# Root at the outputs for two attention linears and the expert queries, and modulation sums moved between linears

## The reference

```python
def rms_norm(x, g):
    y = xf * lax.rsqrt(jnp.mean(xf * xf, axis=-1, keepdims=True) + EPS)
    return y * g
def modulate(h, shift, scale):
    return h * (1 + scale[:, None, :]) + shift[:, None, :]
...
mod = c_act @ ada_w[layer] + ada_b[layer]            # nine vectors: shift, scale, gate three times
h = modulate(rms_norm(x, norm_g[layer, 1]), sh2, sc2)
qkv = h @ w_qkv                                      # layer 0; layer 1 has h @ w_q alone
...
# expert layer, h = rms_norm_2(x, norm_peer_g)
q = jnp.einsum('bsd,dq->bsq', h, w_pq).reshape(b, s, PEER_HEADS, 2, PEER_HALF)
sub_scores = jnp.einsum('bshpc,pnc->bshpn', q, subkeys)
top_s, top_i = lax.top_k(sub_scores, 16)             # then the best 16 of the 16 x 16 pairs, and a softmax
act = jax.nn.gelu(jnp.einsum('chkd,cd->chk', u_sel, hc)) * gc
out = jnp.einsum('chk,chkd->cd', act, v_sel)
```

## Time and profile before

| | us |
|---|---|
| median of 3 runs | 2206.01 (2204.38 to 2207.89) |
| the profiled execution, its own time | 2206.66 |
| its span, first to last instruction | 2204.8 |
| PE busy | 1933.1 (88%) |
| DVE busy | 1680.7 (76%) |
| ACT busy | 878.7 (40%) |
| POOL busy | 531.1 (24%) |
| mean granted TensorE clock | 0.932 of full |

### The profile page before, as it was taken

The page is one execution under the profiler, slowest core; times in us unless marked ns, Lnnn a source line. Parts: engine busy times, 40 slices in busy tenths (PEclk is TensorE's granted clock), DMA queues, the critical chain, the costliest instruction groups (busy, mean ns, idle before and its releaser), DMA issues.

```text
span 2204.8 us, 33666 instructions
## 1 busy us (share of the span) xinstructions
PE 1933.1 (88%) x12770; PEld 1636.5 (74%) x12770; DVE 1680.7 (76%) x2959; ACT 878.7 (40%) x1415; POOL 531.1 (24%) x467
## 2 busy tenths in 40 slices
PE   6999997999999999899999999989876676766766
PEld 6999995999999999699999999979622222222222
DVE  6876877887778768774569998648887787887765
ACT  3444446544454444654545444655321211212111
POOL 0110001211102110111120001423565544445441
PEclk7999996999999999899999999999998888888888
DMA  7878770577848777245444454424999999999996
GB/s 315 309 281 333 298 268 20 192 306 278 288 159 308 282 259 296 81 173 191 154 169 172 174 190 173 172 96 155 390 422 422 422 422 423 422 422 423 422 423 268
DMA packets 88358, 604.80 MB, mean 274 GB/s; under 512 B 9715, under 2 KB 11011, under 8 KB 21036
## 3 DMA queue, kind: packets, MB, share of 16 engines
q1 hardware_dynamic: 37276, 243.46, 30.6%
q0 software_dynamic: 37040, 270.57, 29.5%
q10 hardware_dynamic: 13920, 89.15, 10.4%
HBM read 599.96 MB, written 3.18 MB: 274 GB/s over the span
## 4 chain that ended last, share of the span: by engine, by line
PE 29%; DMA 21%; DVE 7%; ACT 2%; issue 1%; DVEq 0%; ACTq 0%; POOLq 0%
DMA row_pair<-in_peer_uv,mod_ring 21%; PE ps L760 20%; PE ps L1172 3%; PE ps L791 3%; DVE row_pair L2362 2%; DVE w_lo L1708 1%; DVE work L1775 1%; ACT w_hi L1194 1%; PE ps L868 0%; PE ps L986 0%; ACT diag L1675 0%; DVE work L2139 0%; PE ps L823 0%; PE ps L973 0%; DVE work L1963 0%
## 5 line engine op out<-in xcount | busy, mean ns | idle before, releaser
L1708 DVE TENSOR_TENSOR w_lo<-raw,w_hi 128x2048 fp32r<-128x2048 f32 (+1 forms) x248 | 525.5, 2121 | 219.9 <-ACT w_hi L1194 219.3
L1172 PE MATMUL ps<-row_pair,diag 128*128 128x512 f32 x768 | 429.9, 720 | 192.5 <-ACT diag L1675 192.5
L760 PE MATMUL ps<-HH,w_hi 128*128 128x256 f32 x2032 | 575.7, 283 | 1.0 <-DVE w_lo L1708 1.0
L760 PE MATMUL ps<-HL,w_hi 128*128 128x256 f32 x2032 | 571.4, 281 | 0.0
L760 PE MATMUL ps<-HH,w_lo 128*128 128x256 f32 x2032 | 569.1, 280 | 0.0
L1194 ACT ACTIVATE w_hi<-raw 128x2048 fp32r<-128x2048 f32 (+1 forms) x248 | 439.9, 1776 | 264.7 <-PE ps L760 219.8
L1172 PEld LDWEIGHTS ps<-row_pair,diag 128*128 128x128 f32 x768 | 171.2, 230 | 450.5 <-ACT diag L1675 244.3
L2362 DVE SCALAR_TENSOR_TENSOR row_pair<-row_pair,HTOK 128x1024 f32<-128x1024 f32 x256 | 313.7, 1226 | 131.5 <-DMA row_pair<-in_peer_uv,mod_ring 129.3
L733 POOL DMA_INDIRECT row_pair<-in_peer_uv,mod_ring x256 | 318.4, 1244 | 326.1 <-PE ps L1172 261.1
L760 PEld LDWEIGHTS ps<-HH,w_lo 128*128 128x128 f32 x2032 | 383.3, 189 | 0.0
L760 PEld LDWEIGHTS ps<-HL,w_hi 128*128 128x128 f32 x2032 | 382.9, 188 | 0.0
(11 more groups left out here) (311 smaller groups left out, 2926.0 us busy)
## 6 DMA issues: line engine op xcount, KB each, us to landing
raw<-in_f_in SPq DMA_DIRECT2D x88, 1024.0 KB, 4.9
mod_ring<-in_ada ACTq DMA_DIRECT2D x74, 1024.0 KB, 6.6
raw<-in_f_out SPq DMA_DIRECT2D x64, 704.0 KB, 5.0
raw<-in_mix_a SPq DMA_DIRECT2D x16, 1024.0 KB, 4.8
raw<-in_mix_g SPq DMA_DIRECT2D x8, 1024.0 KB, 4.8
raw<-in_pq SPq DMA_DIRECT2D x8, 1024.0 KB, 4.8
first<-in_ada ACTq DMA_DIRECT2D x4, 1024.0 KB, 11.0
raw<-in_a_q SPq DMA_DIRECT2D x4, 1024.0 KB, 7.9
```

Of the source, the lines that this page charges most:

```text
L760: ins = mm(out_, ops[1] if left else ops[0], ops[0] if left else ops[1], start=(first and k == k0 and n == 0), stop=(last and k == k1 - 1 ...
L1172: last = mm(ps[:, 2 * t + c, :], diag[:, d, :], row_v(k)[:, c * 512:(c + 1) * 512], start=False, stop=False)
L1708: v.tensor_tensor(slot(w_lo, g), slot(raw, g), f32(slot(w_hi, g)), ALU.subtract).then_inc(low["v"], 1)
```

## The change

a_q and b_q become raw linears. Their raw tiles are made in `ffn` (with gain/8, which stands for the factor on the queries) and lie in the buffers HH and HL, which the normalised chunks then overwrite one by one, each after tile 1 has read it (`raw_read`). Their outputs are scaled by the new `raw_scale` on DVE, and ACT adds the shift (`raw_take`). The end of `ffn` has no norm sum of its own any more.

The modulation tiles move: 28 and 29 to a_q's tiles 2 and 3, 30 to 33 to a_k, 34 and 35 to a_v, 76 and 77 to b_q's tiles 2 and 3, 78 and 79 to b_o; the sums and takes follow. The loads of the subkeys and the memory on SP's queue move from ahead of f11_in's first tile to behind its third (they wait for the last modulation sum). In s_v, the last two outputs are taken ahead of the last chunk's high and low part. Attention B's small buffer `decay0` moves to the root's place.

In pq all eight tiles run on x times the weight. The sums of squares are made per token (`token_sums`), root and reciprocal are two columns `RT`, and the scores are scaled with them as ACT copies them (L1635). Only x is turned to token-major form; `HTOK` becomes x times `RT` times the weight row, which SP loads twice by broadcast once x_o is done, ahead of pq's tile 3. The cross-attention's output has its parts in EH and EL instead of HH and HL. All of pq is taken by ACT.

```diff
@@ -575,8 +584,16 @@
-            def ffn(w_in, w_out):
+            def memory():
+                sp.wait_ge(mods_ready, summed(ADA_TILES // 2 - 1))
+                sp.dma_start(subk[:, :, :], a["subkT"]).then_inc(sub_loaded, 16)
+                sp.dma_start(MEM, a["memT"]).then_inc(mem_loaded, 16)
+            def ffn(w_in, w_out, late=None):
                 tiles(w_in, 0, RING)
+                if late is not None:
+                    late()
...
@@ -591,12 +608,15 @@
             tiles("b_o")
-            sp.wait_ge(mods_ready, summed(ADA_TILES // 2 - 1))
-            sp.dma_start(subk[:, :, :], a["subkT"]).then_inc(sub_loaded, 16)
-            sp.dma_start(MEM, a["memT"]).then_inc(mem_loaded, 16)
...
+            ffn("f11_in", "f11_out", late=memory)
...
+            tiles("pq", 0, 3)
+            sp.wait_ge(units_done, LIN["x_o"].unit_end)
+            for t in range(TT):
+                sp.dma_start(HTOK[:, t, :], a["norm_peer_row"].partition_broadcast(P).rearrange("q a n -> q (a n)")
+                             ).then_inc(gpeer_loaded, 16)
+            tiles("pq", 3, 5)
...
@@ -713,11 +732,9 @@
                 if n == 1:
-                    pool.wait_ge(hl_ready, SET["n11"] + DC)
-                if n == 2:
+                    pool.wait_ge(el_ready, ESET["attX"] + DC)
+                if n == 3:
                     pool.wait_ge(tok_turned, 4)
-                if n == 3:
-                    pool.wait_ge(tok_turned, 8)
...
@@ -1028,12 +1042,14 @@
+            raw_tile("a_q", 0, 1, mid=lambda: norm_sum(1))
+            raw_tile("a_q", 1, 1, mid=lambda: mod_sum(13))
+            for t in range(2, 4):
+                feat_tile("a_q", t, new="n1", raw=True)
             for t in range(4):
-                feat_tile("a_q", t, new="n1", mid=(lambda: mod_sum(14)) if t == 2 else None)
+                feat_tile("a_k", t, mid=(lambda: mod_sum(14 + t // 2)) if t % 2 == 0 else None)
             for t in range(4):
-                feat_tile("a_k", t, mid=(lambda: mod_sum(15 + t // 2)) if t % 2 == 0 else None)
-            for t in range(4):
-                tok_tile("a_v", t, mid=(lambda: mod_sum(17)) if t == 0 else None)
+                tok_tile("a_v", t, mid=(lambda: mod_sum(16 + t // 2)) if t % 2 == 0 else None)
...
@@ -1068,14 +1084,17 @@
             ffn(2, "f10_in", "f10_out", "n4", 5, 56)
-            for t in range(4):
-                feat_tile("b_q", t, new="n5", mid=(lambda: mod_sum(38)) if t == 2 else None)
-            mod_sum(39)
+            raw_tile("b_q", 0, 5, mid=lambda: norm_sum(5))
+            raw_tile("b_q", 1, 5, mid=lambda: mod_sum(37))
+            for t in range(2, 4):
+                feat_tile("b_q", t, new="n5", raw=True)
             pe.wait_ge(freed["d"], LIN["b_q"].freed_d)
-            pe.wait_ge(mods_ready, summed(ADA_TILES // 2 - 1))
+            pe.wait_ge(mods_ready, summed(37))
             pe.wait_ge(attn_ready, STEP_END["B"])
+            mod_sum(38)
             residual("b_o", "attB", 6)
+            mod_sum(39)
...
-            raw_tile("pq", 0, N_PEER, mid=lambda: norm_sum(N_PEER))
-            raw_tile("pq", 1, N_PEER)
-            head_scores(0)
-            tok_turns(0)
-            for t in range(2, 8):
-                feat_tile("pq", t, new="n11", raw=True, mid=(lambda: head_scores(t - 1)) if t > 2 else None)
-                if t == 2:
-                    head_scores(1)
-                if t < 5:
+            def token_sums():
+                ks = [k for k in range(DC) if not 0 < k < PRE]
+                pe.wait_ge(presum_ready, PRESUM[N_PEER])
+                pe.wait_ge(squares_ready, 8 * RANK[N_PEER] + DC)
+                for t in range(TT):
+                    for k in ks:
+                        last = mm(ps_token[:, t:t + 1], SQ[:, k, t * P:(t + 1) * P], ones[:, 0:1],
+                                  start=(k == ks[0]), stop=(k == ks[-1]))
+                last.then_inc(sumsq_ready, 1)
+            raw_tile("pq", 0, N_PEER, mid=token_sums)
+            for t in range(1, 8):
+                feat_tile("pq", t, mid=lambda: head_scores(t - 1))
+                if t <= TT:
-            pe.wait_ge(tok_ready, 8)
+            pe.wait_ge(tok_ready, 4)
...
@@ -1250,10 +1284,15 @@
                     act.wait_ge(t_ready, 8 * n + k + 1)
+                    if n in EIGHTH and k < DC - 1:
+                        act.wait_ge(raw_read, (DC - 1) * EIGHTH.index(n) + k + 1)
+                    if n in EIGHTH and k == DC - 1:
+                        act.wait_ge(units_done, CHUNK_UNIT[LIN["a_q" if n == 1 else "b_q"].chunk0 + 3])
                         act.wait_ge(units_done, LIN["s_v"].unit_end)
+                        take("s_v", 6, VS[:, 0, 3 * 256:4 * 256])
...
@@ -1461,22 +1500,28 @@
+            split(LIN["a_q"].tile0 + 2)
             shift_high("n1", 1)
+            split(LIN["a_q"].tile0 + 3)
             for t in range(4):
-                split(LIN["a_q"].tile0 + t + 2)
-                if t:
-                    load_mod(28 + t + 1)
+                if t > 1:
+                    split(LIN["a_q"].tile0 + t + 2)
+                if t == 3:
+                    load_mod(30)
                     q = 2 * t + m
-                    take("a_q", q, QT[:, q, :], scale=HD ** -0.5)
+                    if t < RAW_TILES:
+                        raw_take(1, t, q, QT[:, q, :]).then_inc(freed["a"], 1)
+                    else:
+                        take("a_q", q, QT[:, q, :], scale=HD ** -0.5)
                 split(LIN["a_k"].tile0 + t + 2)
-                load_mod(32 + t + 1)
+                load_mod(31 + t)
                 split(LIN["a_v"].tile0 + t + 2)
-                if t == 0:
-                    load_mod(37)
+                if t < 3:
+                    load_mod(35 + t)
...
@@ -1624,37 +1677,31 @@
             split(LIN["pq"].tile0 + 2)
-            norm_root(N_PEER)
-            norm_high(N_PEER)
-            split(LIN["pq"].tile0 + 3)
+            act.wait_ge(sumsq_ready, RANK[N_PEER] + 1)
+            f(RT, ps_token, ACT.Sqrt, scale=1.0 / D, bias=eps[:, :]).then_inc(token_root, 1)
                     f(S[t][:, 2 * h:2 * h + 2, :].rearrange("p a n -> p (a n)"), ps[:, SUBKEY_BANK[t], 0:2 * NK],
-                      ACT.Copy).then_inc(s_ready, 1)
+                      ACT.Copy, scale=RT[:, t:t + 1]).then_inc(s_ready, 1)
-                dst, t = (HTOK, XTOK)[j // 2], j % 2
                     act.wait_ge(tok_turned, 2 * j + half + 1)
-                    f(dst[:, t, half * 512:(half + 1) * 512], ps[:, SUBKEY_BANK[half], :], ACT.Copy).then_inc(tok_ready, 1)
-            sub_copies(0)
-            split(LIN["pq"].tile0 + 4)
-            tok_copies(0)
-            for t in range(2, 8):
-                if t > 2:
+                    f(XTOK[:, j, half * 512:(half + 1) * 512], ps[:, SUBKEY_BANK[half], :], ACT.Copy).then_inc(tok_ready, 1)
+            for t in range(8):
+                if t:
                     split(LIN["pq"].tile0 + t + 2)
+                    if t == 1:
+                        act.wait_ge(token_scale, 1)
+                    sub_copies(t - 1)
                 take("pq", 2 * t, QP[:, 2 * t, :])
-                if t > 2:
-                    sub_copies(t - 1)
                 take("pq", 2 * t + 1, QP[:, 2 * t + 1, :])
-                if t == 2:
-                    sub_copies(1)
-                if t < 5:
+                if 0 < t <= TT:
...
@@ -2021,26 +2081,30 @@
             step(v.tensor_copy(lam_vec[:, 3:4], lam_vec[:, 1:2]))
-            ffn(0, "f00_in", "f00_out", MOD_L0 + 16, 1, 8)
+            ffn(0, "f00_in", "f00_out", MOD_L0 + 16, 1, 8, begin=lambda: raw_begin(1, 20))
+            split(LIN["a_q"].tile0 + 2)
             norm(1, X, "n1", 24)
+            split(LIN["a_q"].tile0 + 3)
             mod_take(13)
+            raw_scale("a_q", 1, "n1")
             for t in range(4):
-                mod_acc_tile(28 + t)
-                split(LIN["a_q"].tile0 + t + 2)
-                if t == 2:
-                    mod_take(14)
+                if t > 1:
+                    split(LIN["a_q"].tile0 + t + 2)
+                    mod_acc_tile(26 + t)
             for t in range(4):
-                mod_acc_tile(32 + t)
                 if t % 2 == 0:
-                    mod_take(15 + t // 2)
+                    mod_take(14 + t // 2)
+                mod_acc_tile(30 + t)
                 split(LIN["a_v"].tile0 + t + 2)
-                if t == 0:
-                    mod_take(17)
+                if t % 2 == 0:
+                    mod_take(16 + t // 2)
+                if t < 2:
+                    mod_acc_tile(34 + t)
...
             norm(5, X, "n5", 68)
+            split(LIN["b_q"].tile0 + 3)
             mod_take(37)
+            raw_scale("b_q", 5, "n5")
             for t in range(4):
-                mod_acc_tile(76 + t)
-                split(LIN["b_q"].tile0 + t + 2)
+                if t > 1:
+                    split(LIN["b_q"].tile0 + t + 2)
+                    mod_acc_tile(74 + t)
```

(61 more changed lines are left out.)

95 lines of the change are left out of this document (59 added, 36 removed).

## The result

| | before | after |
|---|---|---|
| median (range) of 20 runs, us | 2203.3 (2199.1 to 2207.9) | 2209.2 (2204.3 to 2214.2) |
| ratio after/before, 95% interval | | 1.0018 [1.0011, 1.0026] |
| the profiled execution, its own time | 2206.66 | 2206.35 |
| its span | 2204.8 | 2204.5 |

The change made the kernel slower by 0.18%, 4.0 us by the ratio (the medians differ by 5.9); forecast were 1.9 fewer. So the spans say nothing here, and I read the traces by stages: each is the time of PE from the first product of one linear to that of another, in the profiled execution, and from the last mark to the end of the span; f11's row ends at the norm sum inside x_k0's first tile. This table is worked out from PE's timelines.

The account below looks back on a forecast made before the run. Bound: the DMA gather stream once without holes, before it a chain of linears where PE should never wait. Terms +0.5 + 2.9 + 1.3 - 0.7 - 5.9 = -1.9 give 2204.8, median 2204.1; forecast's own range 2200.5 to 2208, stated range 2196 to 2210.5.

Parts of the forecast that it names:

- A: Raw a_q and moved modulation sums, with a new PE wait of 4.3 in a_k: +0.5 us (bounds -5.6 and +1.5).
- B: b_q, attention B and b_o: attention B starts 1.0 later, two modulation sums add 1.9; together +2.9 us.
- D: f11_in, subkey and memory loads late: tile 3 lands later and PE waits, +1.3 us (bounds 0 and +3).
- C: pq: first gather 9.0 earlier, the gather stream runs without holes sooner, -5.9 us (bounds -7.5 and -4).
- E: s_v: PE's wait of 2.0 for DVE's last V copy gets shorter, -0.7 us (-1 to 0).
- half clock: Granted clock of mostly 1.2 GHz after PE idles; 1.8 us assumed behind A's wait in a_k (bounds 0 and 2.6).
- S: Time origin of A's layout: 243.1 us, where PE ends f00_out and, before the change, its norm sum starts.
- Rivals 1 and 2: 1: DVE keeps ahead in a_k, 2198.0 (0.17); 2: DVE no bound in b_q either, about 2188.8 (0.08).
- Rival 3: pq: broadcast loads delay tile 3, or slot reuse holds gathers; C nil, slower, 2210.0 us; chance 0.15.

Follow-up runs that it names:

- e2: Kernel before with parts C, E and A (a_q raw, its sums as in after), without B and D: ratio 0.9976, -5.3 us against before.
- e1: Kernel before with parts C and E alone; a_q, b_q, their modulation tiles and the loads put back: ratio 0.9966, -7.5 us against before.
- e3: Kernel after with the loads of subkeys and memory behind f11_in's tile 8 instead of tile 2: ratio 0.9989, -2.4 us against before.
- e5: Kernel after with sums 14 to 17 one tile later and the subkey and memory loads behind tile 8: ratio 0.9963, -8.1 us against before.
- e4: As e2, with modulation sums 14 to 17 one tile later, in the odd tiles of a_k and a_v: ratio 0.9942, -12.8 us against before.
- e6: Kernel after with the loads of subkeys and memory behind f11_in's tile 3: ratio 0.9989, -2.4 us against before.
- e7: Kernel after with the loads of subkeys and memory behind f11_in's tile 4: ratio 0.9990, -2.2 us against before.
- e10: Kernel after with unused products filling PE's waits ahead of sum 14 in a_k and of f11_in's tile 2: ratio 0.9996, -0.9 us against before.
- e8: As e5, modulation pairs 38 and 39 moved from b_q and b_o to f11_in's tiles 2 to 7, loads behind tile 14: ratio 0.9960, -8.8 us against before.
- e9: As e8, the pairs six tiles later, in f11_in's tiles 8 to 13, loads behind tile 15: median 2190.1 us, ratio 0.9937, -13.9 against before.

## Why the prediction was wrong, point by point

Forecast and measured by part; after is the sum of the differences of neighbouring runs, so the last column adds up to +4.0 by construction, each of its entries is uncertain by some 3 to 4, and the profiles' stages are the independent reading:

| part | forecast | profiles' stages | runs |
|---|---|---|---|
| A | +0.5 | +1.5 | +2.2 (e2 - e1) |
| B | +2.9 | +0.9 and 1.9 | +2.9 (e3 - e2), +4.6 (e5 - e4) |
| D | +1.3 | +6.0 | +6.4 (after - e3) |
| C and E | -6.6 | -7.4 and -0.8 | -7.5 (e1) |
| sum | -1.9 | +2.1 | +4.0 |

The median, 2209.2, lies inside the stated range of 2196 to 2210.5; what was wrong is the direction, slower where the sum said faster.

**D is the step that failed.** Its mechanism was right to the last link (the wait for sum 39 on SP's queue, tile 3 behind the memory, ACT's two splits ahead of the silu that frees the bank), and both its terms were too small. First, the landing: "tile 3 lands at 13.7 and tile 4 at 16.2" were 14.4 and 18.1. The rate wasn't the error, for 422 GB/s were moved, as in the gathers:

```profile
956.00:960.00 4.00, 4.00 (x36) 4.00 (x35) 4.00 (x11) 2.40 (x6) 0.00 (x0) 1.00 1.01 422
960.00:964.00 4.00, 4.00 (x36) 4.00 (x35) 2.26 (x4) 1.92 (x1) 0.00 (x0) 1.00 1.01 422
```

The wait for sum 39 ended at 6.5 and not at 5.7, and SP took 1.2 more to issue the two loads ahead, so tile 3 went out at 7.7. Tiles 3, 4 and 5 followed each other by 0.6, and tile 4 came 3.7 behind tile 3, where a megabyte alone takes 2.5. By then 4.1 MB had been moved since 953.0 (361 GB/s over 11.45 us), 0.8 more than the loads up to tile 4 hold, so tile 5's data was moving along with tile 4's; that this is the reason is worked out from the amounts, and no run tests it. The later landing made the wait 3.2 in place of 1.3. Second, I had given the wait no half clock: the same text that took 1.8 for A's wait of 4.3 took nothing for this one, and its upper bound of +3 left it out too. It was 2.8. e3, e6 and e7 show that the whole 6 hang on where the loads stand; e10 that the half clock hangs on PE's idling, though its profile has only 2 of the 2.8 back by tile 4 and loses them again by the slower pace.

**A** came out in its order of events: DVE ready at S+33.0 (forecast 32.5), PE at 28.9 (28.2), wait 4.2 (4.3), half clock 2.3 (1.8), and 0.44 at tile 3 (0.4). Within the stage that is +1.5 for +0.5: PE came to the sum 0.7 later than forecast, and the half clock was 0.5 longer. That is at the upper bound as stated, +1.5; added up, its terms give only +1.3 (74.0 + 0.4 + 4.3 + 2.6 - 80.0). That a mending was at hand, the same sum one tile later, the prediction doesn't say; e4 has its size, 7.5 by the runs and 6.2 in the stage.

**B** was right in all three terms: attention B 0.9 later (1.0), 9.5 of idle PE ahead of it (9), and two sums on PE's full stretch. The stages b_q to b_o have +3.0 for +2.9, within the scatter named above. e8 and e9 bear out the reason given, that DVE bounds b_q: without two accumulations of 2.8 attention B starts 5.4 earlier.

**C** was right and a little low: first gather 22.0 after pq's start (21.0), gather 6 at 42.2 (43.5), gather 11 at 55.4 (56.6); the part is worth 7.4 in this profile and 5.7 to 8.9 over the eleven kernels that have it, for a forecast of 5.9 (bounds -7.5 and -4). Gather 6 was 1.3 nearer than I had it, which is most of the difference to 7.4.

**E** was right: the wait went from 2.0 to 1.3.

**The rivals.** Rivals 1 and 2 didn't happen: PE waited 4.2 in a_k, and attention B starts 36.0 after f10_out's end and not 27.6. Rival 3 (broadcasts ahead of pq's tile 3) didn't happen: PE has no wait in pq's tiles. That its number, +4.0, is the one measured is luck: it takes C as nil, and C came in full. It had the right kind of mechanism, a load behind a wait on SP's queue, and the wrong place: I asked that question with care where there were 15 us of slack, and in D, where ACT had under 1 to spare (before, the silu in f11_in waited 0.59 for DVE behind the table load and was done 0.3 ahead of PE), gave it one sum. With D at its price and A as measured, the forecast's own sum would have been -1.9 + 4.7 + 1.0 = +3.8, and with C and E by the profiles +2.2: on the side on which the runs fell.

## What to carry to other kernels

Where a transfer is moved behind a wait on a queue, price what stands behind it at the place where it is wanted, with all transfers that are let go together, and add to every new wait of PE the half clock that may follow it, here 2.3 behind 4.2 and 2.8 behind 3.2: it can cost as much as the wait. Short waits aren't safe from it: in e8 the clock fell behind waits of 1.0 and 1.2 us, 4 us apart. A sum or a pair of accumulations that comes right behind a raw tile's scalings finds DVE late (a_k, f11_in, and in all these kernels f01_in); one tile later (a_k) or six (f11_in) it is free or nearly so. And when parts of both signs are put into one change, a kernel for each part pays: of this one C, E and a mended A bring 13 us, while as written it loses 4.
